# A hybrid decoder step on one core: order of the first tiles, second block, turning and page gather; memory kept across stages

## What is computed

```python
def layer(...):
    pp = mix_in(x_p, g_pre, w_in)                 # RMSNorm, then x @ w_in, all head groups
    a_p, pC, pn, pm = mlstm_branch(pp, ...)       # group A: mLSTM, 4 heads x 256, chunkwise
    b_p, pk, pv, pki = dsa_prompt(pp, ...)        # group B: indexer picks 256 keys per query, attention
    pmk, pmv = mem_kv(mem_prompt, g_mem, w_mem_k, w_mem_v)
    c_p = mem_branch(pp, pmk, pmv, ...)           # group C: attention into 256 memory tokens
    y_p = mix_out(x_p, a_p, b_p, c_p, w_out, g_post)   # x + RMSNorm(concat @ w_out)
    ...                                           # the same for the decode tokens, with paged caches
```

## Time and profile before

| what | us |
|---|---|
| median of 3 runs (lowest, highest) | 3281.72 (3278.04, 3282.33) |
| the profiled execution, its own time | 3282.22 |
| its span, first to last instruction | 3280.6 |
| PE busy in it | 3062.9 (93%) |
| DVE, ACT, GpSimd (POOL) busy | 1276.9, 462.7, 406.0 |
| mean granted clock of PE, of full speed | 0.966 |

### The profile page before, as it was taken

How to read it: one execution, slowest core, us unless ns; L and a number is a source line. 1 busy time by engine, 2 the same in 40 slices (tenths; PEclk the granted TensorE clock), 3 DMA queues, 4 the chain that set the end, 5 groups by cost and what they waited for, 6 DMA issues and landing times. The chain is left out here.

```text
span 3280.6 us, 32771 instructions
## 1 busy us (share of the span) xinstructions
PE 3062.9 (93%) x11673; PEld 1613.3 (49%) x11673; DVE 1276.9 (39%) x2331; ACT 462.7 (14%) x981; POOL 406.0 (12%) x567
## 2 busy tenths in 40 slices
PE   6899999999988999999999999999579999479998
PEld 4556666444434444444444444444345565245553
DVE  2201000002212489999999755100132232144553
ACT  2100100011102420000000120000122222012221
POOL 0000000002210000000000046100003200133332
PEclk9999999999999999999999999999789999789999
DMA  5341112233433032021012267300375410666543
GB/s 198 119 88 57 57 56 71 101 111 104 134 130 124 10 116 72 20 71 71 20 70 101 92 201 230 122 20 19 96 270 158 136 46 26 210 169 190 177 147 101
DMA packets 228762, 353.27 MB, mean 108 GB/s; under 512 B 37276, under 2 KB 135428, under 8 KB 223372
## 3 DMA queue, kind: packets, MB, share of 16 engines
q1 hardware_dynamic: 187324, 269.85, 25.0%
q0 software_dynamic: 14784, 61.88, 6.1%
q10 hardware_dynamic: 26544, 20.08, 2.1%
HBM read 267.86 MB, written 86.43 MB: 108 GB/s over the span
## 5 line engine op out<-in xcount | busy, mean ns | idle before, releaser
L270 PE MATMUL sbank<-w,xT 128*128 128x512 f32 x2560 | 1103.9, 594 | 8.4 <-ACT pout_b L249 3.3
L270 PEld LDWEIGHTS sbank<-w,xT 128*128 128x128 f32 x2560 | 486.5, 190 | 620.8 <-issue 612.7
L817 PE MATMUL bank<-w,xT 128*128 128x512 f32 (+3 forms) x2048 | 722.7, 513 | 0.0
L817 PEld LDWEIGHTS bank<-w,xT 128*128 128x128 f32 x2048 | 385.9, 190 | 307.4 <-issue 167.0
L1570 PE MATMUL at_bank_bc<-at_w_bc,at_hT 128*128 128x512 f32 x512 | 230.0, 593 | 3.9 <-ACT at_bc_out L1727 3.9
L2519 PE MATMUL mo_bank_acc<-mo_w_out_a,mo_hT 128*128 128x512 f32 x512 | 232.2, 598 | 0.0
L631 DVE TENSOR_TENSOR area<-area 128x512 f32<-128x512 f32 (+1 forms) x9 | 6.2, 691 | 521.6 <-DMA area<-in_rot 286.8
L244 ACT ACTIVATE pout_b<-sbank 128x512 f32<-128x512 f32 x80 | 47.3, 598 | 992.8 <-PE sbank L270 992.8
L1215 DVE MATCH_REPLACE8 prompt_scores<-m,prompt_scores 128x384 f32<-128x384 f32 (+2 forms) x192 | 165.7, 876 | 0.0
L1212 DVE MAX8 m<-prompt_scores 128x8 f32<-128x384 f32 (+2 forms) x192 | 155.5, 879 | 11.9 <-DVE prompt_scores L1215 11.9
L1570 PEld LDWEIGHTS at_bank_bc<-at_w_bc,at_hT 128*128 128x128 f32 x512 | 94.6, 190 | 103.0 <-issue 101.6
(11 more groups left out here) (363 smaller groups left out, 2793.4 us busy)
## 6 DMA issues: line engine op xcount, KB each, us to landing
w<-in_w_in SPq DMA_DIRECT2D x26, 2048.0 KB, 12.6
proj<-pout_b SPq DMA_DIRECT2D x80, 256.0 KB
w<-in_w_in SPq DMA_DIRECT2D x6, 1376.0 KB, 9.8
area<-in_x_prompt SPq DMA_DIRECT2D x8, 1024.0 KB, 5.7
headT<-area ACTq DMA_DIRECT2D x8, 1024.0 KB, 5.2
prompt_scores<-roped_q_of_decode POOLq DMA_DIRECT2D x32, 256.0 KB
at_w_bc<-in_w_out SPq DMA_DIRECT2D x4, 2048.0 KB, 15.9
y_of_groups_b_c<-at_bc_out SPq DMA_DIRECT2D x32, 256.0 KB
```

What stands on the lines that cost most here:

```text
L270: last = k.nc.tensor.matmul(bank[0:r, 0:self.w], k.xT[:, c, r0:r0 + r], k.w[:, u, c, 0:self.w], start=c == 0, stop=c == KT - 1)
L817: last = nc.tensor.matmul(dst[:, 0:wd], k.xT[:, c, t * P:(t + 1) * P], w[:, b % 2, c, 0:wd], start=c == 0, stop=c == KT - 1)
```

## The change

- `project_rotate`: `keep(0)` ahead of `normalise(1)` and `square(1)`; the first block's weights in four loads, tile 1's rows between the second and third, and PE waits for each quarter as it comes to it. Block 2 of the list is now `C_I + 344`, ahead of the memory blocks; banks are counted from tile 9, and PE waits for the last `keep` at tile 11. `GATES` is 2, `gates.store` four blocks later. `TURNING` hangs the groups of turned heads on full tiles only, up to the last full one.
- `select`: GpSimd waits for the six small loads before it gathers page 1. The eight copies to `kn4`, `vn4` are issued here, and `ahead()`, called once the last but one block is done, loads what attention opens with into the free half of `w` and into `area`.
- `area` (5 x 2048 columns) and `w` are kept across stages and hold other tiles in turn.
- `attend_bc` loads what is left; at slot 33 it loads two of the four blocks of `w_out` for the last stage and `dq`, `dk`.

```diff
@@ Projection.sync
+        sp.wait_ge(self.free, self.n + 1)
+        ahead()
         self.store(sp, self.n - 1, 1, i)
@@ FirstProjection
-    BLOCKS = ([(C_I, 344), (MEM_K, HW), (MEM_V, HW), (C_I + 344, 344), (C_I + 688, 344)] +
+    BLOCKS = ([(C_I, 344), (C_I + 344, 344), (MEM_K, HW), (MEM_V, HW), (C_I + 688, 344)] +
...
-    GATES, MZ, SV, SZ = 3, 8, 9, 10
+    GATES, MZ, SV, SZ = 2, 8, 9, 10
...
+        full = [m for m in range(self.FIRST[self.MZ], self.ALL) if self.TILES[m][1] < QT]
+        self.TURNING = {m: q for q, m in enumerate(full[-2 * N_TILES - 2:-1])}
@@ project_rotate
-            return rbank[m % 2] if m < N_TILES else bank[m % P_BANKS]
+            return rbank[m % 2] if m < N_TILES else bank[(m - N_TILES) % P_BANKS]
...
-            q = m - FIRST_R
+            q = fp.TURNING.get(m, -1)
...
+            def load_first(part):
+                c0, wd = fp.BLOCKS[0]
+                s = slice(4 * part, 4 * part + 4)
+                sp.dma_start(w[:, 0, s, 0:wd], k.w_in_v[:, s, c0:c0 + wd]).then_inc(w_first[part], 16)
...
-            load_w(0)
+            load_first(0)
+            load_first(1)
             load_x(1)
+            load_first(2)
+            load_first(3)
...
             normalise(0)
+            keep(0)
             normalise(1)
-            keep(0)
...
             square(0)
+            keep(0)
             square(1)
-            keep(0)
...
-                if m == N_TILES:
+                if m == N_TILES + 2:
                     pe.wait_ge(kept_a, 2 * ROWS)
                     pe.wait_ge(kept_v, 2 * ROWS)
                 for c in range(KT):
+                    if m == 0 and c % 4 == 0:
+                        pe.wait_ge(w_first[c // 4], 16)
@@ select
+            for t in range(DEC_T):
+                for dst, src in ((k.kn4, outs["sample_k"]), (k.vn4, outs["sample_v"])):
+                    sp.dma_start(dst[t, :, :, :], ...).then_inc(k.new_stored, 16)
+            def ahead():
+                sp.dma_start(k.mk, outs["prompt_mem_k"]...).then_inc(k.mk_in, 16)
+                for b in range(2):
+                    sp.dma_start(k.mkd[:, b, :, :], ins["cache_mem_k"][b]...).then_inc(k.mkd_in[b], 16)
+                for b in range(5):
+                    sp.dma_start(k.mvd[:, 2 * b:2 * b + 2, :], ins["cache_mem_v"][b]...).then_inc(k.mvd_in, 16)
+                sp.wait_ge(k.dots_s, 2 + 2 * NS)
+                sp.dma_start(k.kT, k.headT[:, T_K:T_K + H, 0:SEQ]).then_inc(k.keys_in, 16)
+                sp.dma_start(k.v, outs["prompt_v"]...).then_inc(k.keys_in, 16)
-            pr.sync(sp)
+            pr.sync(sp, ahead)
...
+            pool.wait_ge(const, 16 * 6)
             for p in range(1, 4):
@@ attend_bc
-            sp.dma_start(mk, outs["prompt_mem_k"]...).then_inc(mem_in, 16)
-            sp.dma_start(mv[:, :, :], outs["prompt_mem_v"]...).then_inc(mem_in, 16)
...
+            sp.dma_start(mv[:, :, :], outs["prompt_mem_v"]...).then_inc(mv_in, 16)
-            with sp.Fori(0, DEC_B // 2) as i:
+            with sp.Fori(1, DEC_B // 2) as i:
...
-            for b in range(DEC_B):
+            for b in range(5, DEC_B):
...
+                if s == A_UNITS + 1:
+                    sp.wait_ge(finished, A_UNITS)
+                    sp.wait_ge(m_finished, A_UNITS)
+                    for b in range(2):
+                        sp.dma_start(k.w_a(b), ins["w_out"][0:ML_W, b * O_W:(b + 1) * O_W]...).then_inc(k.w_a_in[b], 16)
+                    for j, c in enumerate((C_Q, C_K)):
+                        sp.dma_start(k.area[0:NS, 8192 + ML_W * j:8192 + ML_W * (j + 1)], ...).then_inc(k.dqk_in, 16)
@@ mix_out
-            sp.dma_start(dq, k.proj[SEQ:TOK, C_Q:C_Q + ML_W]).then_inc(d_in, 16)
-            sp.dma_start(dk, k.proj[SEQ:TOK, C_K:C_K + ML_W]).then_inc(d_in, 16)
...
-            for b in range(O_B):
+            for b in range(2, O_B):
```

More of the change, by code:

```diff
@@ L443, in project_rotate @@
     ROWS = QT + 3
-    FIRST_R = fp.ALL - 22
     with ExitStack() as st:
@@ L2518, in multiply @@
                 for j in range(4 * half, 4 * half + 4):
-                    last = nc.tensor.matmul(acc[n % 2][:, :], hT[:, c % 2, j, :], w[:, j, b * O_W:(b + 1) * O_W],
+                    last = nc.tensor.matmul(acc[n % 2][:, :], hT[:, c % 2, j, :], w[b][:, j, :],
                                             start=j == 0, stop=j == HT - 1)
@@ L2613, in _ @@
                 for b in range(O_B):
-                    last = nc.tensor.matmul(acc0[NS * b:NS * (b + 1), :], hT[:, 0, c, 0:NS], w[:, c, b * O_W:(b + 1) * O_W],
+                    last = nc.tensor.matmul(acc0[NS * b:NS * (b + 1), :], hT[:, 0, c, 0:NS], w[b][:, c, :],
                                             start=c == 0, stop=c == HT - 1)
```

131 lines of the change are left out of this document (74 added, 57 removed).

## The result

Over four executions the changed kernel took 3231.7 us in the median (3219.0 to 3238.4), the kernel before 3282.0 (3278.0 to 3284.5): a ratio of 0.984, 95% interval 0.9825 to 0.9858. The forecast was 3232.0, with a range of 3216 to 3248. The profiled execution took 3229.0 with a span of 3227.3, 53.3 us less than the span of before; the sum had 49.7.

What follows compares the result with a forecast made beforehand. The prediction took PE's few long waits, with slow matmuls behind them, to bound the kernel. Terms 8.0 + 1.5 + 8.1 + 9.0 + 12.1 + 11.0 = 49.7 off 3282.2, less 0.5 for the median, gave 3232.0; range 3216 to 3248.

Steps and rivals of the forecast that it cites:

- First tiles: Start of the program: copies of tile 0 go first, so PE multiplies near 17; 8.0 us, bounds 7.7 and 9.7.
- Second block: Weights for ready rows follow the first block, removing PE's wait before the memory blocks; 1.5 us, bounds 0 and 1.5.
- Turning: Rotated heads: groups on full tiles only remove PE's wait after a short tile; 8.1 us, bounds 5.1 and 9.5.
- Page gather: Start of `select`: six small loads land sooner when POOL's gather waits for them; 9.0 us, bounds 7.1 and 9.7.
- The rival's reasoning: Start of `select`: queues turn packet by packet, so holding the gather brings nothing; 3241 us, chance 0.07.
- Attention: Start of attention: loads issued in `select` shorten waits for `at_lk`, memory keys and values; 12.1 us, bounds 9 and 14.
- Last stage: Unit 4's wait shrinks as 4.46 MB are loaded under attention; 11.0 us, bounds 7.7 and 15, wait left 17.
- Costs with cover: Loads moved earlier in `select`, the last block and attention's end delay others, but cover suffices; cost nothing.
- rival 1: Gates' loads behind larger weights make block 4's weights late; PE waits 4, loses 2 of clock: 3238 us, chance 0.08.

Runs made afterwards that it cites:

- the undoing: Kernel with the gates' loads late (3221.4 us), tile 1 normalised ahead of the copies of tile 0 again, weights still in quarters: 3226.8 us.
- the clean undoing: Kernel with the gates' loads late (3221.4 us), groups of turned heads hung on 22 tiles in a row again, short ones included: 3228.8 us.
- in the second: Changed kernel run once more, nothing edited: median 3219.8 us (3218.7 to 3231.1), profiled execution 3218.7 with no wait for `w`.

## Why the forecast was near, point by point

**First tiles: mis-sized, 11.2 for 8.0.** The order of DVE and ACT was the mechanism, as said, and PE multiplied near 17. The step that failed is "the first half of 7.00 us ends at 24.1": it took 4.86, the clock being up, which had been my upper bound. PE multiplied 8.0 us sooner and took 2.1 less for that half; another 1.0 came from the tiles behind, where the text had put nothing. In six of the twelve traces with the multiplication near 17 the half took 4.9, in six others 6.4 to 6.8, so 2 us of this term are scatter. That tile 1 lands early behind half the weights was seen in the text, but its square was bound to ACT's copies; the undoing shows the quarters worth as much as the order.

**Second block: right by itself (1.7), wrong by what it brought.** The cost at the gates' loads was put at nothing, with 4 us of cover and a chance of 0.08. The step that failed is the size of that cover: I had SP held for 38.5 us and PE waiting only from 42.5. It begins at 39. The four memory tiles took 55.2 us, not 57.0, and the hold is not a constant: 39.5 to 49.5 in five traces with this order, which one trace of before, with 35, can't show. Of the 4.5 to 14.5 us over those 35, some 3.5 are the larger weights ahead, as said, and the rest is the part at 1 GB/s. In the profiled execution it took 3.5 with its slow matmuls; in three of the five traces, all from one chip, PE waited 9 to 11.

**Turning: right.** 8.5 in the first trace, 6.5 to 7.3 by the clean undoing, 8.1 in the sum.

**Page gather: right, small side.** 10.5 for 9.0: `ktn` needed 2.0 us and not 3.5. The rival's reasoning failed at "so a small load would not stay behind a whole gather": the queues do take turns, but one turn of the gather is 32 KB. The gather of before was issued at 972.15, 3 us ahead of the last small load and not "at the same moment", as it says there, and that doesn't change the term.

**Attention: mechanism right, mis-sized.** `at_lk` gave 6.7 (6.6), memory keys 2.6 (2.4), memory values 5.9 for 3.1. The term missing is the clock of the matmuls behind the wait, 2.8, and 1.0 in the loop over keys. I had counted the clock for the turning alone.

**Last stage: right to unit 4, 11.6 for 11.0** (14.7 of wait left, not 17). The bytes were the mechanism for this step; the wait that is left is SP's list as well. Then 3.5 were lost to a later return of the clock, which scatters (22.2 to 28.5 us for the same stretch) and belongs in the range, not in the sum.

**Costs with cover** were nothing, as said, but for the gates' loads. `select` between its start and attention was even 1.4 shorter, the stores at the end of attention were not waited for, and SP's wait in `ahead()` held nobody.

So the sum of 49.7 met 53.3 in the first trace, with rival 1 in it in its small form, and 63.6 in the second, without it (3280.6 - 3217.0), which is above the 59.4 of all upper bounds together. Four terms left their own bounds upwards: 11.2 against 9.7, 1.7 against 1.5, 10.5 against 9.7 and 16.2 against 14. That the median of the first four is within 0.3 us of the forecast is partly chance: terms that were too small were offset in some executions by a cover that was too large. The range held all nine.

## What to carry over

When a load is moved earlier on a queue, read how long the loads ahead of it hold the engine that issues them, and take this from several executions, and several chips, before calling the rest a cover: loads of single elements held it 39.5 to 49.5 us here. When a small load meets a large one on another queue, count packets and not bytes. Give every wait that goes two prices, its length and the slow matmuls behind it (2 to 3 us here). To price one part when times scatter, undo it in a kernel in which the largest cause of the scatter has been taken away, and measure between two marks of the trace.

## What was not expected of the hardware

Small loads (100 bytes to 32 KB) issued while an indirect gather was on its way landed with it, after up to 13 us instead of 2 to 5: the DMA engines gave each queue one packet in turn, 30 and 30 in 2 us, and the gather's were of 32 KB. Two element-wise loads (8448 elements, 33 KB together) and the four small ones behind them held the issuing engine for 39.5 to 49.5 us, about 13 of these while 4.2 MB of weights ahead of them drained and 26 to 36 at about 1 GB/s. After a stall of 16 us in the last stage the granted clock returned for good 10 us after the start of the next unit in one execution and 26 in another, with the same instructions.
